# Token-on-partition norms, respread modulation chunks and an early start in a two-block f32 model kernel

## What is computed

```python
def rms_norm(x, g):
    y = x * lax.rsqrt(jnp.mean(x * x, axis=-1, keepdims=True) + EPS)
    return y * g

def first_block(x, ...):
    h = hybrid_mixer(rms_norm(x, attn_pre_norm), ...)          # norm n1
    x = x + rms_norm(h, attn_post_norm)                        # n2
    h = conv_ffn(rms_norm(x, ffn_pre_norm), ...)               # n3
    return x + rms_norm(h, ffn_post_norm)                      # n4

def second_block(x, c, ctx, ...):
    for l in range(2):
        mod_l = split(silu(c) @ ada_w[l] + ada_b[l], 6)        # chunks ada0, ada1
        h = modulate(x, norm_mix_g[l], mod_l[0], mod_l[1])     # m10 / m10c (context), m11
        x = x + mod_l[2] * mixer(h)
        x = x + mod_l[5] * mlp(modulate(x, norm_mlp_g[l], mod_l[3], mod_l[4]))   # m20, m21
    return rmsnorm(x, final_norm_g)                            # final
```

## Time and profile before

| what | value |
|---|---|
| median of 3 runs | 3070.59 us (3069.9 to 3075.28) |
| the profiled execution: its own time, its span | 3070.38 us, 3068.6 us |
| TensorE matmul busy, weight load busy | 2965.6 us (97%), 2262.1 us (74%) |
| VectorE, GpSimd, ScalarE busy | 1408.9, 874.8, 806.5 us |
| mean granted TensorE clock | 0.984 |
| chain that ended last | 84% TensorE, 7% VectorE, 5% weight load, 2% ScalarE |
| read from HBM | 362.30 MB, 118 GB/s over the span |

### The profile page before, as it was taken

One profiled execution on the slowest core, in us unless ns is written; L12 is line 12 of the kernel. 1 busy time (PEld: TensorE's weight loads), 2 busy tenths in 40 slices (PEclk: granted clock), 3 DMA queues, 4 the chain that ended last, 5 costly groups with the idle time before them and its releaser, 6 DMA issues.

```text
span 3068.6 us, 38419 instructions
## 1 busy us (share of the span) xinstructions
PE 2965.6 (97%) x15252; PEld 2262.1 (74%) x15252; DVE 1408.9 (46%) x2602; ACT 806.5 (26%) x1750; POOL 874.8 (29%) x772
## 2 busy tenths in 40 slices
PE   8999899998999999999999899999999999999998
PEld 7766789997865545555558688888786666678897
DVE  1243278733265635555543443242336555541652
ACT  1022122201023324555620120010103355540210
POOL 0000134584410102122234333443230111110685
PEclk9999999999999899999999999999999999999999
DMA  7454334442345122322222122222331333334442
GB/s 252 154 229 195 123 124 160 158 170 91 110 170 215 55 98 96 110 96 97 83 71 95 69 83 83 84 95 83 110 110 42 108 106 110 110 109 155 142 171 104
DMA packets 65207, 370.15 MB, mean 121 GB/s; under 512 B 6074, under 2 KB 21498, under 8 KB 22672
## 3 DMA queue, kind: packets, MB, share of 16 engines
q1 hardware_dynamic: 48768, 334.60, 30.4%
q10 hardware_dynamic: 15296, 29.56, 3.0%
q0 software_dynamic: 976, 3.63, 0.3%
HBM read 362.30 MB, written 1.28 MB: 118 GB/s over the span
## 4 chain that ended last, share of the span: by engine, by line
PE 84%; DVE 7%; PEld 5%; issue 2%; ACT 2%; PEldq 0%; POOL 0%; DMA 0%; POOLq 0%; DVEq 0%; ACTq 0%
PE PB L476 13%; PE PB L1278 12%; PE PA L476 10%; PE PB L356 8%; PE PS L476 7%; PE PB L1259 6%; PE PB L1012 5%; PE PB L1117 3%; PE PB L1292 3%; PE PB L400 2%; PE PA L1361 2%; PE PA L1330 1%; PE PA L1344 1%; PEld PB L476 1%; PEld PB L576 1%
## 5 line engine op out<-in xcount | busy, mean ns | idle before, releaser
L1278 PE MATMUL PB<-H,ring 128*128 128x512 f32 (+1 forms) x1024 | 428.8, 567 | 0.0
L511 POOL TENSOR_TENSOR sums<-ring 128x512 f32<-128x512 f32 x115 | 152.8, 1328 | 637.0 <-PE PA L476 262.6
L1278 PEld LDWEIGHTS PB<-H,ring 128*128 128x128 f32 x1024 | 192.3, 191 | 185.5 <-issue 180.1
L476 PE MATMUL PB<-work,sums 128*128 128x128 f32 (+1 forms) x1360 | 230.5, 327 | 0.0
L476 PEld LDWEIGHTS PB<-work,sums 128*128 128x128 f32 x1360 | 207.0, 191 | 17.6
L476 PE MATMUL PA<-work,sums 128*128 128x128 f32 (+1 forms) x1280 | 208.9, 318 | 0.0
L2764 POOL TENSOR_TENSOR work<-work 128x256 f32<-128x256 f32 x96 | 59.8, 644 | 518.4 <-ACT work L1782 416.5
L476 PEld LDWEIGHTS PA<-work,sums 128*128 128x128 f32 x1280 | 187.4, 191 | 13.6
L620 DVE TENSOR_TENSOR work<-PA,work 128x128 f32<-128x128 f32 (+1 forms) x53 | 18.9, 357 | 382.6 <-ACT work L604 382.6
L2426 DVE SCALAR_TENSOR_TENSOR work<-PB,par,work 128x510 f32<-128x510 f32 (+3 forms) x256 | 181.7, 713 | 24.1 <-ACT work L1760 17.3
L1012 PE MATMUL PB<-H,ring 128*128 128x256 f32 (+1 forms) x640 | 177.3, 432 | 0.4 <-DVE rstd L2075 0.2
(11 more groups left out here) (361 smaller groups left out, 5327.8 us busy)
## 6 DMA issues: line engine op xcount, KB each, us to landing
ring<-stream SPq DMA_DIRECT2D x315, 1024.0 KB, 4.8
sums<-cs_rows ACTq DMA_DIRECT2D x16, 1024.0 KB, 4.7
sums<-cs_rows ACTq DMA_DIRECT2D x16, 512.0 KB, 3.8
work<-work ACTq DMA_DIRECT2D x16, 256.0 KB, 4.5
work<-scratch POOLq DMA_DIRECT2D x1, 2560.0 KB, 15.1
X<-xT SPq DMA_DIRECT2D x2, 1024.0 KB, 13.2
out<-H SPq DMA_DIRECT2D x1, 1024.0 KB, 4.8
con<-consts SPq DMA_DIRECT2D x1, 652.0 KB, 18.0
```

The source lines that it names most:

```text
L476: mm = pe.matmul(fast_bank(side, bank)[:, col:col + width], weight(k), right(4 * part + k), start=first and opens and k == 0, stop=last an ...
L511: nc.gpsimd.tensor_tensor(su[:, 0], a21, a22, ALU.add).then_inc(sem("w_summed"), 1)
L1278: mm = pe.matmul(PB[:, pair, t, 0:Tc], ring[:, c % SLOTS, k, t * P:(t + 1) * P], H[:, k, 0:Tc], start=(k == 0), stop=(k == KT - 1))
```

## The change

Four things. (1) Norms other than n1: the squares become the stationary operand, so that the mean of a token stands on the token's partition; root and reciprocal work on 128x2 (128x4 for 512 columns); two (four) matmuls by the identity, `norm_spread`, put the result back on all partitions in PSUM, where DVE reads it. For n2, n3 and n4 (`COPIED`) it is spread twice and ScalarE copies the second to `RSTD`, for POOL and the late scaling. DVE's products of `residual1` go to PSUM. (2) Start and end: first loads are cut in halves; TensorE does chunk 0 on tiles without 1/rms (columns 256:512 of `H` as a scratch place), sums n1 between its halves, and DVE applies 1/rms as it evacuates; the output is stored in four pieces. (3) `ada0` chunks go to 24 of the 32 units, those where u % 8 is neither 1 nor 4. (4) `halves_chunk` and the first chunk of `pe_features` with a `ready` go k by k, both halves t of each tile in turn. Also: `X_ORDER` is another, three semaphores of DVE's fast sums become one.

```diff
+ADA_AT = [i for i in range(A_UNITS) if i % 8 not in (1, 4)]
-                + ([("ada0", u)] if u < ADA_CHUNKS else []) for u in range(A_UNITS)]
+                + ([("ada0", ADA_AT.index(u))] if u in ADA_AT else []) for u in range(A_UNITS)]
...
+                    first = ready and j == skip
+                    for t, k in [(t, k) for k in range(KT) for t in range(2)] if first else \
+                            [(t, k) for t in range(2) for k in range(KT)]:
...
 def norm_sums(pe, tag, T, sq, tiles, at=0):
+                for t in range(T // P):
+                    mm = pe.matmul(sums_to(tag)[:, t * P:(t + 1) * P], sq(k)[:, t * P:(t + 1) * P], full(ONE_D),
+                                   start=(i == 0 and t == 0), stop=(i == KT - 1), skip_group_check=True)
...
-        def norm_root(act, tag, step, half=0, col=0):
+        ROOT = small[:, 96:100]
+        def norm_root(act, tag):
+            nc.scalar.activation(ROOT[:, 0:n], sums_to(tag)[:, 0:n * P:P], ACT.Sqrt, bias=EPS_C).then_inc(sem("norm_root"), 1)
+            if tag in COPIED:
+                act.wait_ge(sem("norm_spread_twice"), COPIED.index(tag) + 1)
+                nc.scalar.activation(RSTD[:, 0:T1], PS[:, 1, 0:T1], ACT.Copy).then_inc(sem("norm_copied"), 1)
+        def norm_rstd(v, tag):
+            nc.vector.reciprocal(ROOT[:, 0:n], ROOT[:, 0:n]).then_inc(sem("norm_inverse"), 1)
+            v.wait_ge(sem("norm_spread"), SUMMED.index(tag))
+        def norm_spread(pe, tag):
+            pe.wait_ge(sem("norm_inverse"), SUMMED.index(tag) + 1)
+            for t in range(n):
+                mm = pe.matmul(sums_to(tag)[:, t * P:(t + 1) * P], full(ROOT[:, t:t + 1]), ident, start=True, stop=True)
+            mm.then_inc(sem("norm_spread"), 1)
+            if tag in COPIED:
+                for t in range(n):
+                    mm = pe.matmul(PS[:, 1, t * P:(t + 1) * P], full(ROOT[:, t:t + 1]), ident, start=True, stop=True)
+                mm.then_inc(sem("norm_spread_twice"), 1)
...
 sync
-            sp.dma_start(X[:, :, 0:T1], xT[:, :, 0:T1]).then_inc(sem("x_landed"), 16)
-            sp.dma_start(ring[:, 0, :, :], stream[0]).then_inc(landed[0], 16)
-            sp.dma_start(par[:, :], params).then_inc(loaded, 16)
+            sp.dma_start(par[:, g_at:g_at + KT], params[:, g_at:g_at + KT]).then_inc(sem("first_landed"), 16)
+            sp.dma_start(X[:, 0:4, 0:T1], xT[:, 0:4, 0:T1]).then_inc(sem("first_landed"), 16)
+            sp.dma_start(ring[:, 0, 0:4, :], stream[0, :, 0:4, :]).then_inc(sem("first_landed"), 16)
+            sp.dma_start(X[:, 4:KT, 0:T1], xT[:, 4:KT, 0:T1]).then_inc(sem("x_landed"), 16)
+            sp.dma_start(ring[:, 0, 4:KT, :], stream[0, :, 4:KT, :]).then_inc(landed[0], 16)
+            sp.dma_start(par[:, KT:N_PARAMS], params[:, KT:N_PARAMS]).then_inc(loaded, 16)
...
+            for k in range(0, KT, 2):
+                sp.wait_ge(sem("final_h"), k + 2)
+                sp.dma_start(out[:, k:k + 2, :], H[:, k:k + 2, 0:T1]).then_inc(sem("stored"), 16)
...
 tensor
+            for t in range(2):
+                for k in range(KT):
+                    if t == 0:
+                        pe.wait_ge(sem("n1_h"), k + 1)
+                        if k == 4:
+                            pe.wait_ge(landed[0], 16)
+                    mm = pe.matmul(PB[:, pair, t, 0:T1], ring[:, 0, k, t * P:(t + 1) * P], H[:, k, T1:TT],
+                                   start=(k == 0), stop=(k == KT - 1))
+                if t == 0:
+                    norm_sums(pe, "n1", T1, lambda k: SQ[:, k, 0:T1], range(KT))
...
                     def q_ready(n, k):
+                        if n == 0 and k == 4:
+                            norm_spread(pe, "n4")
                         if n == 1 and k == 0:
                             norm_sums(pe, "m10", T1, lambda k: SQ[:, k, 0:T1], X_ORDER)
+                            norm_spread(pe, "m10")
...
 vector, residual1
+                tiles = [bank[:, T1 * i:T1 * i + T1] for bank in (PS[:, 0], PB[:, free, 1], PA[0]) for i in range(2)]
-                        vec.tensor_tensor(src[:, k, :], src[:, k, :], RSTD[:, 0:T1], ALU.mult)\
+                        vec.tensor_tensor(tiles[i], src[:, k, :], root_of(tag), ALU.mult).then_inc(sem(f"{tag}_part"), 1)
-                        vec.tensor_tensor(x1(k), x1(k), src[:, k, :], ALU.add).then_inc(sem(f"{tag}_x_dve"), 1)
+                        vec.tensor_tensor(x1(k), x1(k), tiles[i - 1], ALU.add).then_inc(sem(f"{tag}_x_dve"), 1)
```

More of the change, by code:

```diff
@@ L280, in program @@
         SUMMED = ["n1", "n2", "n3", "m10c", "n4", "m10", "m20", "m11", "m21", "final"]
-        ROOTED = ["n1", "n2", "n3", "m10c", "n4", "m10", "m20", "m20b", "m11", "m11b", "m21", "final"]
+        COPIED = ["n2", "n3", "n4"]
         def past(tag):
@@ L692, in norm_added @@
                     squared(pe, tag, k + 1)
[L693 removed]
+                for t in range(T // P):
+                    mm = pe.matmul(sums_to(tag)[:, t * P:(t + 1) * P], sq(k)[:, t * P:(t + 1) * P], full(ONE_D),
+                                   start=(k == 0 and t == 0), stop=(k == tiles[-1]), skip_group_check=True)
             mm.then_inc(sem("norm_sum"), 1)
```

167 lines of the change are left out of this document (98 added, 69 removed).

## The result

| | before | changed kernel |
|---|---|---|
| median of the runs, us | 3072.94 (4 runs, 3069.9 to 3075.55) | 3031.51 (4 runs, 3028.8 to 3036.76) |
| profiled execution: time, span | 3070.38, 3068.6 | 3028.8, 3026.9 |
| mean granted TensorE clock | 0.984 | 0.994 |
| sum of stretches at the lower clock (1.2 GHz) | 102 us | 40 us |

The ratio of after to before is 0.987, 95% interval 0.9857 to 0.9882: faster by 41 us. 3037.5 was forecast, with a range of 3028 to 3050. The two profiled executions differ by 41.6 us, the two medians by 41.4.

The account below looks back on a forecast made before the run. TensorE was busy 97%, so only its waits and lower-clock time could be won: 4.2 + 12.5 + 5.0 - 0.4 + 7.0 + 2.0 + 2.6 = 32.9 us off 3070.4 gave 3037.5 us, range 3028 to 3050.

Parts of the forecast that it names:

- Start: Kernel start: chunk 0 begins on half loads before the n1 sums and ends sooner; gain 4.2 us, bounds 3 and 5.2.
- plus 0.4: Start: 0.4 us added to 24.2 - 20.5 = 3.7 for the bias table's matmul, which stood ahead of chunk 0 before.
- Units of kind c: First attention, 265 to 315.3 us: moved `ada0` chunks cover waits and keep the clock up; gain 5.9 + 6.6 = 12.5 us.
- rival B: Clock falls all the same in kind-c units and behind m10; price 6.6 + 2.5, 3046.6 us, range 3045 to 3053; chance 0.20.
- the sign set for it: Kind-c stretch: a clock of 0.50 there would show the forecast wrong and the clock falling all the same.
- By tiles: `halves_chunk` and first chunks, k by k: helps only where tiles come slower than 0.434 us; DVE takes 0.41; gain 0.
- n2, n3: Norms n2 and n3: narrow root and reciprocal, DVE steps at 0.4 us, n3 sums sooner; gain 5.0 us, bounds 4 and 6.
- n4, m10: 709.9 to 737.5 us: DVE starts later but steps faster, m10's matmuls end sooner; gain 7.0 us, bounds 4 and 8.5.
- Rival D: Norms: DVE with PSUM inputs no faster beside POOL than 0.94 us; 3046.5 us, up to 3055 with late load; chance 0.05.
- m20, m11, m21: Spreads replace 256-column root and reciprocal: 0.3, 0.5 and 1.2 us, lost clock kept; together 2.0 us, bounds 0 and 5.
- End: Kernel end: scaling starts 0.65 us earlier, last quarter's store lands 1.95 us sooner; gain 2.6 us, bounds 0.7 and 3.8.
- Rival C: Shorter waits keep the clock up behind m20, m11, m21 too, earlier at start; 3030 us, down to 3024; chance 0.10.

Follow-up runs that it names:

- the run with matmuls ahead: Changed kernel plus seven unused 256-column TensorE matmuls ahead of the wait for the first loads; 3039.2 us, ratio 0.989.
- the waits filled: Matmuls with overwritten results where TensorE waits: added to the changed kernel, 3025.02 us; the same edit in the kernel before, 3055.03 us.
- halves apart: Changed kernel with first chunks and chunks by halves taking all eight tiles for one output half, then the other; 3048.57 us, ratio 0.9918.

## Why the prediction was right, and where not

- **Start, 4.2 predicted, 2.5 measured.** The first matmul came 0.9 us later than taken. Some 2.6 us were lost at the lower clock, as taken, and that it was the clock is shown by the run with matmuls ahead. The sum also counts the bias table's matmul wrongly: 20.5 already holds it, and before it ran while TensorE waited for chunk 0, so the "plus 0.4" counts it twice; it took 0.75 us, not 0.4.
- **Units of kind c, 12.5 predicted, 4.6 measured,** below the lower bound of 6. The failed step is "1.07 us covers every 0.5 us wait for the copy, and puts off the next turn by 1.07 us: its waits of 0.7 to 1.8 us shrink to 0 to 0.7", and with it the clock that would "stay up". Of 5.9 us of waits 1.2 were gained, of 6.6 us of clock 3.4. Waits for copies shrank; a turn behind a gate chunk still waited up to 1.8 us. Where no chunk stood between, a chunk there took 1.0 us off the wait, as the run with a chunk in each unit shows. The last unit's wait did not move in any run but those that filled it with work. Why DVE is late there was only argued: it works in order, and evacuates the gate half first. The clock, low three times before (from 271.8, 285.4 and 312.7 us), fell once, from 303.0, over the last turn and the first branch chunk. That is half of rival B, and the sign set for it came.
- **By tiles, 0 predicted, 4.4 measured by its waits,** and up to 1.7 us of clock behind the first. This is the step that was wrong in kind. I costed it from norms, where tiles come in 0.41 us, and did not look for other waits of first chunks. The list of TensorE's waits before had both, 2.4 and 1.6 us, under the line that this part changes. A missing row, not a wrong price: 2.4 in the attention, 2.0 at `out20n`.
- **n2, n3: 5.0 and 4.4. n4, m10: 7.0 and 6.6.** Right, and by the reason given: DVE's steps at 0.4 us, n4 starting later and ending sooner. Rival D did not come, and its price was fair: with root and products in SBUF, 0.94 us a step, nearly all of the gain is gone.
- **m20, m11, m21: 2.0 predicted, 5.3 measured.** The starts came to 2.4 (0.5, 0.7 and 1.2). The other 2.9 us are clock on balance, 2.1 of it in m21 (9.27 to 7.14), which the step said would be kept. Most other traces do lose it, so this is luck of the execution.
- **End: 2.6 and 3.6.** The store is worth 2.5 (I took the line between two sizes, 1.95; the landing of 256 KB is 2.3), the norm 1.0 (I took 0.65).
- **Not in the sum: 7.4 us at L1449**, clock alone, and luck: the run with one store, which differs in its last lines only, does not have it. Rival C had "the clock stays up" at 0.10, but in other places.

So the total was right in part by luck, by terms that erred both ways: 7.9 us too much in the units, 4 to 6 too little for the order by tiles, and some 10 us of clock unforeseen (7.4 at L1449, 2.9 behind m20, m11 and m21). Split as the traces are, the forecast has about 10 us of clock (6.6 in the units, 0.5 at n3, 2.6 behind m10) and 23 of work; measured were 19 of clock and 23 of work, or 13 and 19 with the waits filled. The work came out near the forecast only because the units gave 4.7 us less in waits than priced and the order by tiles 4.4 more.

## What to carry to other kernels

Before pricing a part at nothing, go through every wait of the engine that is listed under the lines it touches; two waits of 4 us in all stood there. An addition or product on VectorE that runs beside GpSimd's was twice as fast here with one input in PSUM (0.42 us for 0.94). And where TensorE waits for a known time, matmuls into a bank that is overwritten anyway delayed nothing here: 27 of them gave 6.5 to 10 us and runs that repeat within 3 us, about as much as the largest part of the change. Do it first. Until then the falls of the clock move from one execution to the next, by up to 12.6 us in the same kernel, so that a difference of that size in the total can be the clock alone; read the stage.

## What the runs showed of the hardware

- The clock can fall in a stretch where TensorE is mostly busy, and stay low while it is busy without a pause. From 996 to 1014.5 us of the changed kernel TensorE is busy 15.2 of 18.5 us, with waits of at most 1.2, all of them ahead of 1006.4; in 4 of 14 traces (before, halves apart, one store, a chunk in every unit) the clock fell 3.4 to 5.0 us ahead of this projection and stayed at 1.2 GHz for 20.5 to 23.9 us, through its 32 matmuls of 64 columns (64 records) in a row. In the others it fell for 3.4 us or not at all. It did not fall in the three traces with filled waits.
- Two operands decide what VectorE and GpSimd cost each other. 128x256 f32 on VectorE beside GpSimd: 0.42 us with an input in PSUM; with both in SBUF 0.62 when every second operation has one in PSUM, 0.94 when none has, 1.48 beside GpSimd on 512 columns, and 0.42 with GpSimd idle. GpSimd's own addition goes from 0.73 to 0.90 us.
- An addition with an input in PSUM took no longer than one from SBUF, 0.41 to 0.42 us both.
- A store of 256 KB landed in 2.3 us and one of 1 MB in 4.8, four small ones in a row included.
